# The last of twelve expert passes with the former pass' down products among its gate products, and the last layer's choices added ahead of the late products

## The chip, the cores and the metric

One Trainium2 chip, one NeuronCore. The core has TensorE (PE, matrix products and transposes into the PSUM banks), VectorE (DVE), ScalarE (ACT), GpSimd (POOL) and SyncE (SP), each with an instruction stream of its own, and DMA queues that the streams feed. The streams meet only at semaphores. The metric is the device time of one launch in microseconds (us), as the median of several runs.

## The reference

A two-layer encoder over 528 positions (16 meta tokens and 512 frames) of width 1024: a retention layer, then a sliding-window attention layer, each followed by a mixture of 16 experts, and a final norm.

```python
def hier_moe(h, w_group, w_router, w_gate, w_up, w_down):
    ...
    weights = g_w * top_p / jnp.sum(top_p, axis=-1, keepdims=True)
    expert_idx = g_sel[:, None] * EXPERTS_PER_GROUP + top_i
    gates = jnp.sum(jax.nn.one_hot(expert_idx, N_EXPERTS, dtype=jnp.float32) * weights[..., None], axis=1)
    a = jnp.einsum('td,edf->tef', t, w_gate)
    u = jnp.einsum('td,edf->tef', t, w_up)
    hid = jax.nn.silu(a) * u * gates[:, :, None].astype(t.dtype)
    y = jnp.einsum('tef,efd->td', hid, w_down)
    return y.reshape(b, l, d)

def reference(...):
    ...
    for i in range(DEPTH):
        ...
        h = h + hier_moe(rms_norm(h, moe_norm[i]), ...)
    return rms_norm(h, final_norm)[:, CHUNK:]
```

So each position goes through two experts of one group, and `h` receives both results, each times its weight.

## The kernel before

Each layer's expert stage sends every position's normed row to two slots of a table in DRAM (`slot_rows`), sorted by expert. The slots are worked off in twelve passes (`ROUNDS` = 12, `PASSES`), each of 128 slots in up to four tiles of 32. A slot group is a "pair" (64 slots of one expert) or a "single" (32 more). The last pass, k = 11, holds four singles, and pass 10 holds two pairs.

A pass k is four pieces of PE work: `rows_to_features(k)` (8 transposes of the slot rows), `gate_up(k)` (L1083: 8 blocks of 128 features, 4 products each, gate and up halves side by side in one bank, 2 or 3 by turns), `hidden_to_features(k)` (L1090: 2 transposes of the hidden values into bank 5) and `down_project(k)` (L1102: 16 products into banks 6 and 7). The trace has two records for each of these products. Between them, ACT makes the tanh of the gate half (`tanh_of`, L1423), DVE the hidden values (`hidden`, L1914 and L1915), ACT copies the transposed hidden values (`hidden_of`, L1436), and the results are copied to `yo` half by ACT (`results_of`, L1444, bank 6), half by DVE (L1923, bank 7). ACT then stores them to the DRAM table `slot_out` (L1450), except for the last pass. PE runs the passes one step apart: gate_up(k), hidden_to_features(k-1), rows_to_features(k+1), down_project(k-1).

The last pass' results are never stored. Instead `late_results` (L1135) multiplies them on PE by a one-hot matrix with the weights in it, one tile of positions after the other (meta tile first in the first layer, then 0 to 3), and DVE adds that to `h` (`add_late`, L1956). All other results are gathered back from `slot_out` by POOL (L2215, an indirect DMA for each of the two choices of each tile, into `gat`), once the stores of passes 9 and 10 have landed. DVE adds them with their weights (`first_choice` and `second_choice`, L1940 through `weighted`). The buffers of the gathered rows of tiles 2 and 3 lie over memory that expert weights used; before tile 3's gathers POOL waits for the last down products (bank 7).

POOL's stream is one queue: after the gathers of tile 2 it waits in the first layer for the square sum of the meta tile and makes its 1/rms (L2147, L2150, `deviations`), and only then gathers for tile 3. In the first layer DVE's order after the passes is: late add of the meta tile, its two choices, late adds of tiles 0 and 1, norm of the meta tile (L1556), first choice of tile 0, features of the meta tile for the keys and values (`kv_features`, L1562), second choice of tile 0, both choices of tile 1, norm of tile 0, and so on. PE goes on with the transposes of the normed tiles (L833) and the key and value products (`key_values`, L1149); tile 0's transposes stand halfway through the meta tile's products. In the last layer DVE adds the late product of tile t+1 behind the choices of tile t; ACT's square sum (L1287), POOL's 1/rms and DVE's final norm (L2121) follow for each tile, and SP stores the output.

SP loads, during the passes, the experts' next weights: the down weights of pass 10 (L684) go out when down_project(8) is done. In the first layer's last pass SP also issues the small tables of the attention stage (L799, `attention_loads`), once gate_up(11) and down_project(10) are both done. POOL has conditional weight loads of its own (L680, L684) that stand ahead of its gathers.

## Time and profile before

| | |
|---|---|
| median of 3 runs | 1138.62 us (1138.2 to 1141.27) |
| profiled execution | 1140.07 us, of which its span is 1138.4 us |
| mean granted TensorE clock | 0.972 |
| PE busy | 1050.2 us, 92% of the span |
| DVE / ACT / POOL busy | 446.1 / 263.5 / 240.5 us |
| chain that ended last | PE 79%, DVE 12%, issue 3%, DMA 2%, ACT 2%, POOL 1% |
| last pass and what follows, first layer | from 668.95 us to 757 us of the span |
| last pass and what follows, last layer | from 1091.92 us to the end |

The shares of the chain tell which engine's work the end waited for. PE holds most of it, but the two places that the change touches lie where the chain leaves PE: after the last pass of each layer it goes through a store, gathers, DVE and ACT. Those stretches are read there, row by row. A row of the timeline gives the start, the duration, the engine, the line and what ended the idle time ahead of it in brackets.

### The profile page before, as it was taken

What the parts mean: (1) busy time and instruction counts of PE and PEld (TensorE: products, weight loads), DVE (VectorE), ACT (ScalarE), POOL (GpSimd) and SP (SyncE); (2) the same over time, 40 slices, a digit from 0 to 9 for tenths busy, and PEclk for the clock granted to TensorE, in tenths of its full rate; (3) what the DMA queues carried; (4) which work ended last, traced back from release to release, by engine and by line L of the source; (5) the groups of instructions that cost most, each with busy time, mean ns of one, the idle gap of its engine ahead of it and who ended that gap; (6) DMA issues with size and microseconds to landing.
All of it is one profiled execution on the core that took longest, in us unless ns stands there. A gap on an engine that the chain in (4) does not pass through costs nothing.

```text
span 1138.4 us, 16440 instructions
## 1 busy us (share of the span) xinstructions
PE 1050.2 (92%) x6553; PEld 662.3 (58%) x6553; DVE 446.1 (39%) x806; ACT 263.5 (23%) x528; POOL 240.5 (21%) x232
## 2 busy tenths in 40 slices
PE   4999999999999999978999998989998978999982
PEld 4989979989988877753333332454444443333321
DVE  6400314224226540155132226557547745232216
ACT  5132143134224411020011111314214510111111
POOL 5333314205214533003000005510000002000004
PEclk9999999999999999988999998989999998999997
DMA  7232223114115121367899887030004058998945
GB/s 305 74 130 75 75 90 114 56 42 161 56 37 168 37 74 74 148 278 285 313 358 376 353 361 259 42 148 0 1 1 148 1 233 339 333 380 323 403 189 222
DMA packets 34838, 201.01 MB, mean 177 GB/s; under 512 B 4352, under 2 KB 4352, under 8 KB 25808
## 3 DMA queue, kind: packets, MB, share of 16 engines
q1 hardware_dynamic: 21168, 151.26, 34.7%
q10 hardware_dynamic: 8864, 31.74, 7.9%
q0 software_dynamic: 4736, 17.04, 4.1%
q8 instruction: 48, 0.79, 0.3%
q14 instruction: 22, 0.18, 0.0%
HBM read 303.70 MB, written 28.44 MB: 292 GB/s over the span
## 4 chain that ended last, share of the span: by engine, by line
PE 79%; DVE 12%; issue 3%; DMA 2%; ACT 2%; POOL 1%; SPq 0%; POOLq 0%; DVEq 0%; ACTq 0%
PE ps L844 30%; PE ps L1083 15%; PE ps L1102 7%; PE ps L969 4%; PE ps L1207 4%; PE ps L1149 3%; PE ps L850 3%; DVE arena L2079 2%; PE ps L1071 2%; DVE arena L2076 2%; PE ps L1060 1%; PE ps L912 1%; ACT arena L1522 1%; PE ps L1167 1%; DMA ring<-in_w_ret 1%
## 5 line engine op out<-in xcount | busy, mean ns | idle before, releaser
L844 PE MATMUL ps<-x_hi,ring_r 128*128 128x264 f32 x1024 | 190.9, 287 | 3.2 <-DVE xT L1562 3.1
L2159 POOL TENSOR_TENSOR ring_r<-ring,ring_r 128x1024 fp32r<-128x1024 f32 x56 | 136.9, 2459 | 260.5 <-ACT ring_r L1299 260.4
L844 PEld LDWEIGHTS ps<-x_hi,ring_r 128*128 128x128 f32 x1024 | 160.3, 190 | 3.6 <-issue 3.3
L1083 PE MATMUL ps<-arena,xT 128*32 128x512 f32 x864 | 158.0, 600 | 0.0
L1083 PE MATMUL ps<-ring,xT 128*32 128x512 f32 x672 | 143.9, 602 | 5.9 <-DVE xT L1562 5.9
L844 PE MATMUL ps<-xT_r,ring_r 128*128 128x264 f32 x512 | 146.2, 286 | 0.0
L1562 DVE TENSOR_TENSOR xT<-ps,gains 128x512 f32<-128x512 f32 (+1 forms) x76 | 46.9, 660 | 182.8 <-PE ps L1071 177.3
L844 PE MATMUL ps<-ring_r,x_hi 128*128 128x512 f32 x320 | 100.6, 395 | 0.0
L844 PEld LDWEIGHTS ps<-xT_r,ring_r 128*128 128x128 f32 x512 | 97.0, 189 | 0.1
L1102 PE MATMUL ps<-arena 128*32 128x512 f32 x624 | 87.3, 595 | 4.3 <-ACT arena L1436 4.3
L1299 ACT ACTIVATE ring_r<-ring 128x1024 fp32r<-128x1024 f32 x56 | 57.9, 1054 | 118.4 <-PE ps L844 70.8
L1083 PEld LDWEIGHTS ps<-arena,xT 128*32 128x32 f32 x864 | 41.6, 111 | 54.9 <-issue 54.4
L1083 PEld LDWEIGHTS ps<-ring,xT 128*32 128x32 f32 x672 | 38.1, 111 | 60.8 <-issue 60.3
L844 PEld LDWEIGHTS ps<-ring_r,x_hi 128*128 128x128 f32 x320 | 60.1, 188 | 13.9
L2147 POOL TENSOR_SCALAR var<-ss 128x1 f32<-128x1 f32 (+1 forms) x23 | 8.5, 371 | 239.7 <-ACT arena L1287 231.6
L1167 PE MATMUL ps<-ring,xT 128*128 128x512 f32 x128 | 56.1, 595 | 0.0
L1287 ACT ACTIVATE arena<-h 128x1024 f32<-128x1024 f32 (+1 forms) x23 | 24.3, 1057 | 102.7 <-DVE h L1940 48.0
L1436 ACT ACTIVATE arena<-ps 128x256 f32<-128x256 f32 x24 | 9.2, 385 | 167.5 <-PE ps L1090 162.9
L969 PE MATMUL ps<-arena 128*128 128x264 f32 (+4 forms) x256 | 47.8, 334 | 0.0
L1102 PEld LDWEIGHTS ps<-arena 128*32 128x32 f32 x624 | 22.8, 109 | 42.9 <-issue 41.3
L1522 ACT ACTIVATE arena<-arena 128x256 f32<-128x256 f32 x64 | 31.6, 494 | 62.6 <-DVE arena L2084 62.6
L969 PEld LDWEIGHTS ps<-arena 128*128 128x128 f32 (+1 forms) x256 | 41.1, 189 | 6.8
(265 smaller groups left out, 1554.7 us busy)
## 6 DMA issues: line engine op xcount, KB each, us to landing
arena<-in_w_gu SPq DMA_DIRECT2D x22, 2048.0 KB, 14.8
ring<-in_w_gu SPq DMA_DIRECT2D x20, 2048.0 KB
arena<-in_w_down SPq DMA_DIRECT2D x36, 1024.0 KB
arena<-in_w_gu POOLq DMA_DIRECT2D x18, 2048.0 KB
ring<-in_w_gu POOLq DMA_DIRECT2D x14, 2048.0 KB
arena<-in_w_down POOLq DMA_DIRECT2D x26, 1024.0 KB
ring<-in_w_ret SPq DMA_DIRECT2D x48, 512.0 KB, 3.7
ring<-in_w_ret_out SPq DMA_DIRECT2D x16, 512.0 KB, 4.9
```

Source lines behind the costliest of these rows:

```text
L844: last = mm(dst, a_parts[x], b_parts[y], start=(start and n == 0), stop=(stop and n == 2))
L850: last = mm(dst, both, part, start=(start and n == 0), stop=(stop and n == 1))
L969: last = mm(ps[:, b + g, c - lo:HALF], v_tm[0:r, t, 128 * m:128 * m + 128], scores_of(t)[0:r, c - 128 * t:hi - 128 * t], start=(t == 0), s ...
L1083: last = mm(ps[cols, b, :], xgT[:, k % 2, c, cols], by_row(gu(j))[:, c, :], start=(c == 0), stop=(c == KT - 1))
L1102: last = mm(ps[cols, b, :], hidT[:, c, cols], down(j)[:, c, 512 * n:512 * n + 512], start=(c == 0), stop=(c == 1))
L1149: last = mm(ps[0:rows(t), b, :], xTk[:, k, col0(t):col0(t) + rows(t)], w_kv[:, k, :], start=(k == 0), stop=(k == KT - 1))
L1167: last = mm(ps[:, b, :], xT[:, k, col0(t):col0(t) + 128], w_q[c][:, k, :], start=(k == 0), stop=(k == KT - 1))
L1207: last = mm(ps[:, b + c, :], oT1[:, k, :], w[:, k, :], start=(k == 0), stop=(k == KT - 1))
L1299: nc.scalar.activation(w_hi[to][:, m], w_raw[slot][:, m], ACT.Copy).then_inc(hi_made, 1)
L1522: nc.scalar.activation(P[:, hd, :], P[:, hd, :], ACT.Exp, bias=nmx[:, hd:hd + 1], accum_out=sm[:, hd:hd + 1]).then_inc(p_exp, 1)
L1562: return V_.tensor_tensor(dst[:, 4 * g:4 * g + 4, c0:c0 + r], src, gains[:, gain, 4 * g:4 * g + 4].unsqueeze(2).to_broadcast([128, 4, r]), ...
L2159: G.tensor_tensor(w_lo[slot][:, m], w_raw[slot][:, m], w_hi[to][:, m], ALU.subtract).then_inc(lo_made, 1)
```

## The change

Four edits, in both layers unless said otherwise.

1. PE's last pass is written in another order. Its gate products come in three pieces: blocks 0 to 2, then hidden_to_features(10), blocks 3 and 4, then down_project(10), then blocks 5 to 7. The pass' bank is told full after the last of them.
2. ACT and DVE follow: ACT makes the last tanh after it has stored pass 10's results, and DVE makes the last hidden values after it has copied pass 10's half.
3. In the last layer DVE adds both choices of a tile first and its late product behind them, so that the square sum of ACT waits for the late add. Before the late add DVE waits for its own second choice.
4. POOL waits for the last gate products (bank 3) before the gathers of tile 2.

```diff
@@ gate_up and the order of PE's passes
-                def gate_up(k):
+                def gate_up(k, blocks=range(KT)):
                     b = gu_bank(k)
-                    weights_arrived(pe, gu_in, gu_again, l, k)
-                    round_read(pe, l, B_ROWS, k)
-                    if k >= 2:
-                        round_read(pe, l, b, k - 2)
-                    for c in range(KT):
+                    if blocks[0] == 0:
+                        weights_arrived(pe, gu_in, gu_again, l, k)
+                        round_read(pe, l, B_ROWS, k)
+                        if k >= 2:
+                            round_read(pe, l, b, k - 2)
+                    for c in blocks:
...
-                    last.then_inc(full[b], 1)
+                    if blocks[-1] == KT - 1:
+                        last.then_inc(full[b], 1)
...
                 for k in range(1, ROUNDS):
+                    if k == ROUNDS - 1:
+                        gate_up(k, range(0, 3))
+                        hidden_to_features(k - 1)
+                        gate_up(k, range(3, 5))
+                        down_project(k - 1)
+                        gate_up(k, range(5, KT))
+                        break
                     gate_up(k)
                     hidden_to_features(k - 1)
@@ ACT
                     hidden_of(k - 1)
-                    tanh_of(k)
+                    if k < ROUNDS - 1:
+                        tanh_of(k)
                     results_of(k - 1)
+                    if k == ROUNDS - 1:
+                        tanh_of(k)
...
-            squares(MOE_TILES[1], nrm["_f"], next_junk, lambda t: act.wait_ge(mo[1]["gath_used"], t + 1))
+            squares(MOE_TILES[1], nrm["_f"], next_junk, lambda t: fl.wait_read(act, f"LC1_{t}"))
@@ DVE
+                    if k == ROUNDS - 1:
+                        results_of(k - 1)
                     hidden(k)
-                    results_of(k - 1)
+                    if k < ROUNDS - 1:
+                        results_of(k - 1)
...
                     dve.wait_ge(m[f"gathered{t}"], 32)
-                    fl.wait_read(dve, f"LC{l}_{t}")
+                    if l == 0:
+                        fl.wait_read(dve, f"LC{l}_{t}")
...
-            add_late(0)
             for t in range(NT):
                 first_choice(t)
                 second_choice(t)
-                if t + 1 < NT:
-                    add_late(t + 1)
+                dve.wait_ge(mo[1]["gath_used"], t + 1)
+                add_late(t)
                 if t == 1:
                     final_norm(0)
@@ POOL
                     r = rows(t)
+                    if t == 2:
+                        round_full(pool, l, gu_bank(ROUNDS - 1), ROUNDS - 1)
                     if t == NT - 1:
                         round_full(pool, l, B_YB, ROUNDS - 1)
```

How PE's order moves, in the last layer's last pass (the first layer's is the same). Lines 1083, 1090 and 1102 of before are 1084, 1092 and 1104 of after; `ring` and `arena` hold the weights. Before, from the last of the eight gate blocks on:

```order
L1083 MATMUL ps<-ring,xT 32x512
L1083 MATMUL ps<-arena,xT 32x512 x3
L1090 MATMUL ps<-con,arena 128x128 [waits bank_free2]
L1090 MATMUL ps<-con,arena 128x128
L1102 MATMUL ps<-arena 32x512 [waits bank_free5,bank_free6,down_in3,down_in2]
L1102 MATMUL ps<-arena 32x512
L1102 MATMUL ps<-down_rows,arena 32x512 x2
```

After, from the third of the eight gate blocks on:

```order
L1084 MATMUL ps<-ring,xT 32x512
L1084 MATMUL ps<-arena,xT 32x512 x3
L1092 MATMUL ps<-con,arena 128x128 [waits bank_free2]
L1092 MATMUL ps<-con,arena 128x128
L1084 MATMUL ps<-ring,xT 32x512
L1084 MATMUL ps<-arena,xT 32x512 x3
L1084 MATMUL ps<-ring,xT 32x512
L1084 MATMUL ps<-arena,xT 32x512 x3
L1104 MATMUL ps<-arena 32x512 [waits bank_free5,bank_free6,down_in3,down_in2]
```

The transposes of pass 10's hidden values and its down products have moved ahead of the last three gate blocks, and two gate blocks stand between them.

DVE's order in the last layer, from its last pass to the second tile. Before:

```order
L1914 SCALAR_TENSOR_TENSOR arena<-arena,ps 128x256 [waits tanh_done_1]
L1915 SCALAR_TENSOR_TENSOR arena<-arena,ps 128x256 [waits dve_steps_moe1]
L1923 COPY arena<-ps 128x512 [waits y_out0_1,bank_full7]
L1923 COPY arena<-ps 128x512 [waits y_out1_1,bank_full7]
L1956 TENSOR_TENSOR h<-ps,h 128x1024 [waits bank_full0,final_gain_in]
L1940 SCALAR_TENSOR_TENSOR h<-arena,h 128x1024 [waits bank_free0,gathered0_1]
L1940 SCALAR_TENSOR_TENSOR h<-arena,h 128x1024 [waits dve_steps_moe1]
L1956 TENSOR_TENSOR h<-ps,h 128x1024 [waits bank_full2]
```

After:

```order
L1935 COPY arena<-ps 128x512 [waits y_out0_1,bank_full7]
L1926 SCALAR_TENSOR_TENSOR arena<-arena,ps 128x256 [waits tanh_done_1]
L1927 SCALAR_TENSOR_TENSOR arena<-arena,ps 128x256 [waits dve_steps_moe1]
L1935 COPY arena<-ps 128x512 [waits y_out1_1,bank_full7]
L1955 SCALAR_TENSOR_TENSOR h<-arena,h 128x1024 [waits gathered0_1,final_gain_in]
L1955 SCALAR_TENSOR_TENSOR h<-arena,h 128x1024 [waits dve_steps_moe1]
L1972 TENSOR_TENSOR h<-ps,h 128x1024 [waits bank_full0,gath_used_1]
```

Pass 10's copy now stands ahead of the last hidden values, and the first late add behind the first tile's choices.

## Rows read from the trace of the kernel before

**Rows 1.** Chain that ended last, first layer: start us, us, what

```profile
668.95 6.87 PE ps L1083 x64
...
681.34 5.75 DMA slot_out<-arena
```

**Rows 2.** Timeline of SP, first layer's last pass: start, duration, engine, line, operation

```profile
680.62 0.33 SPq L799 DMA_DIRECT2D arena<-in_t_swa  x1
```

**Rows 3.** Timeline of POOL behind the first layer's store

```profile
687.89 0.87 POOL L2215 DMA_INDIRECT xT<-slot_out,slot_g  x1 [6.56 <-DMA slot_out<-arena]
...
697.87 0.18 POOL L2147 TENSOR_SCALAR var<-ss 16x1 f32<-16x1 f32 x1
...
698.88 2.67 POOL L2215 DMA_INDIRECT arena<-slot_out,slot_g  x1 [0.19 <-issue]
```

**Rows 4.** Timeline of DVE behind the first layer's passes

```profile
688.90 1.21 DVE L1956 TENSOR_TENSOR h<-ps,h 16x1024 f32<-16x1024 f32 x1 [2.17 <-PE ps L1135]
691.92 2.58 DVE L1940 SCALAR_TENSOR_TENSOR h<-xT,arena,h 16x1024 f32<-16x1024 f32 x2 [1.80 <-DMA xT<-slot_out,slot_g]
694.43 2.34 DVE L1956 TENSOR_TENSOR h<-ps,h 128x1024 f32<-128x1024 f32 x2
698.73 0.74 DVE L1556 TENSOR_SCALAR arena<-h,rstd 16x1024 f32<-16x1024 f32 x1 [1.97 <-POOL rstd L2150]
...
705.19 0.75 DVE L1556 TENSOR_SCALAR arena<-h,rstd 128x1024 f32<-128x1024 f32 x1 [0.46 <-POOL rstd L2150]
```

**Rows 5.** Timeline of ACT there: the meta tile's square sum

```profile
694.53 1.06 ACT L1287 ACTIVATE arena<-h 16x1024 f32<-16x1024 f32 x1 [9.60 <-DVE h L1940]
```

**Rows 6.** Timeline of PE there: late products, transposes, key and value products

```profile
686.99 8.94 PE L1135 MATMUL ps<-arena,short 128*16 128x512 f32 x20 [1.00 <-DVE arena L1923]
699.62 1.00 PE L833 MATMUL ps<-con,arena 16*128 16x16 f32 x8 [3.69 <-DVE arena L1556]
701.16 5.91 PE L1149 MATMUL ps<-ring,arena 128*16 128x512 f32 x8 [0.54 <-DVE arena L1562]
707.00 1.09 PE L833 MATMUL ps<-con,arena 128*128 128x128 f32 x8
```

**Rows 7.** Stretches there: us, busy by engine, PE clock, DMA share, GB/s

```profile
699.00:700.00 1.00, 0.38 (x4) 0.41 (x5) 1.00 (x2) 0.00 (x0) 1.00 (x1) 0.51 0.86 348
```

**Rows 8.** Line 684, 640 to 712 us: the load of pass 10's down weights and its landing

```profile
L684 SPq DMA_DIRECT2D down_rows<-in_w_down x1: 747/747/747, 658.2 to 658.2; - x1
...
DMA to landing us min/median/max: 11.1/11.1/11.1
```

**Rows 9.** Chain that ended last, last layer

```profile
1091.92 6.87 PE ps L1083 x64
1098.79 0.38 PE ps L1090 x2
...
1099.84 3.67 PE ps L1102 x32
...
1104.31 2.61 DMA slot_out<-arena
...
1108.98 6.77 DMA arena<-slot_out,slot_g
```

**Rows 10.** Timeline of the last layer's last pass, PE, ACT and DVE

```profile
1099.48 0.38 ACT L1423 ACTIVATE arena<-ps 128x256 f32<-128x256 f32 x1
...
1100.34 0.42 DVE L1915 SCALAR_TENSOR_TENSOR arena<-arena,ps 128x256 f32<-128x256 f32 x1
...
1105.32 0.63 PE L1102 MATMUL ps<-arena 128*32 128x512 f32 x3 [1.48 <-ACT arena L1436]
```

**Rows 11.** Timeline of DVE, last layer: choices, late add, final norm of the first tile

```profile
1115.78 2.60 DVE L1940 SCALAR_TENSOR_TENSOR h<-arena,h 128x1024 f32<-128x1024 f32 x2 [2.54 <-DMA arena<-slot_out,slot_g]
...
1118.30 1.22 DVE L1956 TENSOR_TENSOR h<-ps,h 128x1024 f32<-128x1024 f32 x1
...
1123.29 1.28 DVE L2121 SCALAR_TENSOR_TENSOR arena<-h,rstd,arena 128x1024 f32<-128x1024 f32 x1
```

## The prediction

> **What bounds the kernel now.** I read the page first: PE is busy for 92% of the span and holds most of the chain that ended last, so what moves other engines matters only where that chain leaves PE. The chain, followed in order of time, leaves it at two places that the change touches: behind pass 10's down products in the first layer [rows 1] and in the last [rows 9]. In both it goes DVE copy, store of pass 10, POOL's gathers, DVE. From there I read the timelines of each engine [rows 2 to 6, 10, 11]. The reader should see three things. In the first layer PE stands idle for 3.69 us between the late products and the transposes of the meta tile, and the products behind that run slowly, 5.91 us for 8 records [rows 6], at a granted clock of 0.51, the lower of the two levels (1.2 GHz), reached in that idle time [rows 7]. What ended the idle time is the meta tile's norm on DVE, which waited for POOL's 1/rms [rows 4], and POOL came to that only when eight gathers were out: 687.89 to 697.87, 9.98 us [rows 3]. In the last layer DVE waits for the first gather until 1115.78 and is then busy nearly without a gap to the end [rows 11].
>
> **The last pass on PE.** I take the last layer's times; the first layer's pass is the same, 422.97 earlier (668.95 against 1091.92) [rows 1, 9]. The eight gate blocks take 6.87, so 0.86 each. Before: gate 1091.92 to 1098.79, transposes 0.38, down products of pass 10 from 1099.84, 3.67 long, to 1103.51 [rows 9]. So 0.67 of stall stood ahead of them, for ACT's copy of the hidden values. After: three blocks 2.58, transposes 0.38, two blocks 1.72 (which hide ACT's copy, 0.67), so the down products start at 1096.6 and end at 1100.2 to 1100.3: **3.3 us earlier**. No row shows a bank left with an open sum while others are written, except the meta tile's key and value products, with another tile's transposes in their middle [rows 6]; nothing stands idle there, so I take nothing for it (0 to 0.3).
>
> The last three blocks end at 1102.8. Now the hidden values of pass 11 have no cover. From the tanh's start to their end is 1.28 (1099.48 to 1100.34 + 0.42) [rows 10], some 0.2 passes until PE starts, and transposes, copy and wait take 1.05 as before (1098.79 to 1099.84) [rows 9]: the last down products start at 1105.4, against 1105.32 [rows 10]. Two stalls of PE, 0.67 and 1.48 [rows 10], have been exchanged for one of 1.5 and one of 0.67. **PE: +0.1 us.** ACT now has the store ahead of the tanh; the store is issued at 1101.0, 1.8 before the tanh can run, so that costs nothing, unless the copies of banks 6 and 7 come 1.5 later.
>
> **The store and the gathers.** The store followed the down products' end by 0.80 (1103.51 to 1104.31) [rows 9], so it goes out at 1101.0 in the last layer and at 678.0 in the first. In the last layer it took 2.61 [rows 9]; in the first 5.75 [rows 1], after SP had issued the attention tables at 680.62 [rows 2], ahead of the store at 681.34. SP waits for the last gate products too, which now end at 679.9, so the tables go out 1.9 after the store instead of 0.7 before it. Its length is between 2.61 and 5.75; I take 2.61, since the tables come last now. First gather 0.80 after landing (681.34 + 5.75 = 687.09 to 687.89) [rows 1, 3]: at 681.4, or 684.6 at the other end, against 687.89.
>
> POOL's new wait for the last gate products (679.9) is over before the first gather; the wait for the last down products (682.4 + 3.7 = 686.1) before it gets to tile 3. Both are free.
>
> **First layer, on DVE.** The late add of the meta tile moves by PE's +0.1 to 689.0 and ends at 690.2. The two choices began at 691.92 after 1.80 of idle, waiting for the gather [rows 4], 4.03 after the first gather's start. With the new start that landing is 685.4 to 688.6, in either case before DVE is free, so they run from 690.2 to 692.7 and DVE does the two late adds until 695.05. Beside it ACT makes the square sum, 1.06 and some 0.2 around it [rows 5], till 693.95; POOL is through its eight gathers at 691.4 (or 694.6) and takes 0.86 (697.87 to 698.73) [rows 3, 4]: 694.8 (or 695.5). So the meta tile's norm runs at 695.1 instead of 698.73, now bound by DVE's own queue. PE started 0.89 after that norm (699.62) [rows 4, 6]: 696.0. The late products end at 686.99 + 8.94 + 0.1 = 696.0 [rows 6]: PE's idle time is gone, and that is also the limit of what can be got there.
>
> Next is tile 0. DVE needs 6.46 from the meta norm to tile 0's norm (698.73 to 705.19) [rows 4], which comes at 701.55, and PE can start tile 0's transposes 0.89 later, at 702.45. PE itself would be there earlier: without the idle time the clock should stay at the upper level, and 8 records then take 8 x 0.447 = 3.6 (8.94 over 20 records) [rows 6] instead of 5.91, so from 697.55 to 701.1. Against 707.00 [rows 6] the gain is **4.5 us**. If the clock falls all the same, PE is there at 703.5: 3.5. If DVE is quicker than before, 701.1 is the floor: 5.9. From here on to 757 us PE works without a gap in the chain, so what is gained is kept.
>
> **Last layer, on DVE.** The first gather landed at 1108.98 + 6.77 = 1115.75 [rows 9]. Everything ahead of it moves by 3.3, the load of the final gains too, so 1112.45. Then DVE has, tile by tile, two choices 2.60 and a late add 1.22 [rows 11], and one final norm in between. Before, three late adds lay behind the first landing, since the first one was done while DVE waited; now four do: +1.22. The new waits for DVE's own second choice cost what the wait between two choices costs, which is next to nothing (2.60 for two) [rows 11]: 0.1 to 0.4 for four. The first late product was added before DVE's idle time began, at 1115.78 - 2.54 - 1.22 = 1112.0 [rows 11], and the others follow 1.8 apart (8.94 for five) [rows 6]; now the first add comes at 1115.1 and they 3.8 apart, so none is late. Together +1.4, net **1.9 us** gained. What follows the last tile (square sum, 1/rms, final norm, store) is as before.
>
> **The sum** is 4.5 + 1.9 = 6.4 us. The profiled execution took 1140.07, so it would be 1133.7; that execution lay 1.45 above the median of 1138.62, and against the median the forecast is **1132.2**. The ends of the terms: first layer 3.2 to 5.9, last layer 1.3 to 2.3.
>
> **A rule weighed against a row.** In the first layer tile 3's gather took 2.67, with DVE's norm of the meta tile beginning 0.15 earlier [rows 3, 4]. The Trainium skill, "SBUF — State Buffer", section "Who interferes with whom", says that a DVE tensor_scalar in its two-port mode and GpSimd lock each other out, and that "Issue order, not op shape, decides who blocks". The long gather agrees with that. Now POOL is done with the 1/rms at 694.8 and issues tile 3's gather at once, ahead of the norm, which waits for DVE until 695.1. By that rule the norm would have to wait for the gather.
>
> **The rivals.** (B) That turn of order costs the meta norm what it cost the gather: 2.67 against the 0.87 of a quick one [rows 3], up to 1.8, once. The sum is 4.6: 1134.0. (C) In the first layer gathers and tables crowd each other, and the meta tile's gathers land no earlier than 691.9: only the clock and part of POOL's queue are gained, 2: 1134.7. For it speaks that the store was slow in such company [rows 1, 2], against it that the meta tile's gathers are small (16 rows) and have until 690.2, 8.8 us from their start. (D) In the last layer the landings of the gathers are set by other traffic, so DVE gains nothing there and pays the 1.4: 4.5 - 1.4 = 3.1: 1135.5. Against it: the traffic before the gathers is that of before, 3.3 earlier. (E) Slower: pass 10's down products stand 3.2 us earlier, and their weights are not there. They landed at 658.2 + 11.1 = 669.3 [rows 8] and are wanted at 673.6, so there are 4.3 us to spare. Beyond that each us s stalls PE, in both layers, since gate blocks and the last down products queue behind: 6.4 - 2s. No gain is left at s = 3.2, and the kernel is slower by more than 0.3% from s = 4.9, say 1142.2 at s = 5. Nothing new is loaded, so this would need a much later landing than this trace has. (F) The change doesn't do what it says, since another wait than PE's order holds pass 10's results (the store of pass 8, bank 7): all went by without idle time in the passes before; 1138 to 1140.
>
> **How the numbers follow.** Forecast 0.68, B 0.10, C 0.10, D 0.07, E 0.03, F 0.02. The range goes from the upper ends of the terms (1138.62 - 8.2 = 1130.4) to a little over D: 1130.3 to 1136.0. With 0.3% (3.4 us, about what a measurement of this kernel can tell from no change) the line lies at 1135.2. Nearly all of the forecast and B, half of C and D are below it: faster 0.85, same 0.12, slower 0.03.
>
> **What the profile of the changed kernel would show.** Pass 10's down products start 4.7 after the last gate products' start, and the last pass as a whole ends within 0.2 of before. Both stores are issued 3.3 earlier and both take about 2.6. In the first layer PE's idle time between late products and meta transposes is under 0.5, the clock stays at 1.00 in that stretch, and 8 records of the key and value products take 3.6. In the last layer the first choice starts 20.5 us after the last pass' gate products, and the last late add ends 16.7 us later, with no idle time of DVE over 0.1 in between. I would be wrong if the store took 5 us in the last layer, if the meta norm still waited for POOL, or if DVE in the last layer waited for gathers of tiles 1 to 3.

## The result, and the profile after

| | before | after |
|---|---|---|
| median of 5 runs each | 1138.2 us (1137.3 to 1141.27) | 1133.22 us (1131.95 to 1133.78) |
| profiled execution | 1140.07 us, span 1138.4 | 1133.78 us, span 1132.1 |
| mean granted TensorE clock | 0.972 | 0.973 |
| PE / DVE busy | 1050.2 / 446.1 us | 1051.0 / 446.2 us |

The ratio is 0.9946, with a 95% interval of 0.9932 to 0.9959: 5 us or 0.5% faster. Between the two profiled executions the span fell by 6.3 us, against 6.4 in the forecast. The medians fell by 5.0. The total is close, but the first layer gave about a microsecond less and the last layer about a microsecond more than forecast, and these cancel. To see it, each stretch is timed from the start of the last pass' gate products of its layer (S0 in the first, S1 in the last), since S0 itself varies by up to 3.3 us between profiles of kernels that are alike up to there. S0 and S1 are the starts of the first gate record in PE's timeline (668.77 and 1091.74 before, 668.87 and 1088.47 after); the chain puts that start 0.2 later, and the forecast's 4.7 counts from there.

| us from S0, first layer | before | forecast | after |
|---|---|---|---|
| pass 10's down products start | 8.1 | 4.7 | 4.8 |
| late products start | 18.2 | 18.3 | 19.7 |
| store of pass 10 is issued | 12.6 | 9.2 | 9.3 |
| first gather | 19.1 | 12.6 to 15.8 | 13.2 |
| meta tile's choices | 23.2 | 21.4 | 23.4 |
| meta tile's norm | 30.0 | 26.3 | 28.2 |
| tile 0's transposes | 38.2 | 33.7 | 35.8 |
| S1 - S0 | 423.0 | 418.5 | 419.6 |

| us from S1, last layer | before | forecast | after |
|---|---|---|---|
| first gather | 16.0 | 12.7 | 12.7 |
| first choice | 24.0 | 20.7 | 19.8 |
| last square sum starts | 39.2 | 37.3 | 36.2 |
| end of the span | 46.7 | 44.8 | 43.6 |

So the first layer gave 3.4 instead of 4.5, and the last 3.0 instead of 1.9. Of the 3.4, only 2.5 was there at tile 0's transposes, where the forecast had its 4.5. The chain that ended last of the kernel after, first layer, in order of time (start, us, engine or DMA, tile and line); lines 1104, 1955, 1972 and 2232 of after are 1102, 1940, 1956 and 2215 of before:

```profile
669.05 2.58 PE ps L1084 x24
...
673.85 3.48 PE ps L1104 x32
...
678.13 3.13 DMA slot_out<-arena
...
683.24 9.05 DMA xT<-slot_out,slot_g
692.31 1.28 DVE h L1955
...
697.27 2.67 POOL arena L2232
...
703.75 0.76 DVE arena L1568
```

The store now takes 3.13 instead of 5.75 [rows 1], but behind it the chain holds a 9.05 us transfer that it did not hold before: the meta tile's second gather, 64 KB. DVE's timeline there:

```profile
690.48 1.21 DVE L1972 TENSOR_TENSOR h<-ps,h 16x1024 f32<-16x1024 f32 x1 [2.17 <-PE ps L1144]
692.31 2.58 DVE L1955 SCALAR_TENSOR_TENSOR h<-xT,arena,h 16x1024 f32<-16x1024 f32 x2 [0.62 <-DMA xT<-slot_out,slot_g]
...
697.11 0.74 DVE L1568 TENSOR_SCALAR arena<-h,rstd 16x1024 f32<-16x1024 f32 x1
```

The choices begin at 692.31, later than the 691.92 of [rows 4], although the gather was issued 5.8 earlier. DVE still waits for the gather there. Only the wait for POOL's 1/rms (1.97 in [rows 4]) is gone: the norm of the meta tile has no idle time ahead of it. What was in the gather's way shows in the DMA issues of 676 to 706 us (KB each, median us from issue to landing). Before:

```profile
arena<-in_swa_b_o SPq DMA_DIRECT2D x1, 512.0 KB, 8.7
...
xT<-slot_out,slot_g POOLq DMA_INDIRECT x2, 3.1
```

After:

```profile
arena<-in_swa_b_o SPq DMA_DIRECT2D x1, 512.0 KB, 10.1
...
xT<-slot_out,slot_g POOLq DMA_INDIRECT x2, 8.3
```

The attention tables, 1.8 MB issued by SP at 680.0 to 682.0, now fall on the gathers instead of on the store. The last table was issued at 682.00, landed 10.1 later at 692.1. Of the meta tile's two gathers the first, issued at 682.06, landed at 689.6, and the second, for which the choices wait, at 692.3.

The other error is on PE. Its timeline in the first layer's last pass and behind it:

```profile
681.27 0.44 PE L1092 MATMUL ps<-con,arena 128*128 128x128 f32 x2 [1.41 <-DVE arena L1927]
682.37 1.08 PE L1104 MATMUL ps<-arena 128*32 128x512 f32 x3 [0.67 <-ACT arena L1445]
...
684.05 1.10 PE L1104 MATMUL ps<-arena 128*32 128x512 f32 x3
...
685.65 0.62 PE L1104 MATMUL ps<-arena 128*32 128x512 f32 x3
...
688.56 8.94 PE L1144 MATMUL ps<-arena,short 128*16 128x512 f32 x20 [1.01 <-DVE arena L1935]
698.00 0.64 PE L833 MATMUL ps<-con,arena 16*128 16x16 f32 x8 [0.50 <-DVE arena L1568]
699.46 3.59 PE L1158 MATMUL ps<-ring,arena 128*16 128x512 f32 x8 [0.82 <-DVE arena L1574]
704.65 1.07 PE L833 MATMUL ps<-con,arena 128*128 128x128 f32 x8 [1.59 <-DVE arena L1568]
```

The two stalls, 1.41 and 0.67, are those of the forecast. What came on top is that the first four of the eight groups of last down products take 0.93 to 1.10 for three records instead of 0.63 [rows 10], because the clock fell. Stretches of the kernel after (us, busy by engine in the order PE, PEld, DVE, ACT, POOL with how many instructions, PE clock, DMA share, GB/s):

```profile
682.00:683.00 1.00, 0.63 (x4) 0.23 (x8) 0.00 (x0) 0.12 (x1) 0.87 (x1) 0.56 0.77 299
683.00:684.00 1.00, 1.00 (x8) 0.23 (x4) 0.00 (x0) 0.00 (x0) 0.77 (x1) 0.50 0.36 124
...
686.00:687.00 1.00, 1.00 (x16) 0.27 (x8) 0.00 (x0) 0.50 (x1) 0.69 (x2) 1.00 0.84 234
...
699.00:700.00 1.00, 0.54 (x2) 0.22 (x3) 1.00 (x4) 0.00 (x0) 0.94 (x1) 1.00 0.00 0
```

From 0.56 at 682 to 0.50 and back to 1.00 at 686: the lower level, 1.2 GHz, for some 3.5 us. The last row answers to [rows 7]: there, where before the clock was at 0.51, it is now up, and the meta tile's 8 records take 3.59 instead of 5.91 [rows 6].

In the last layer the chain reads:

```profile
1097.73 2.61 DMA slot_out<-arena
...
1101.13 0.97 POOL arena L2232
1102.40 5.71 DMA arena<-slot_out,slot_g
1108.22 1.29 DVE h L1955
...
1123.40 1.23 DVE h L1972
1124.66 1.06 ACT arena L1296
```

and DVE's timeline:

```profile
1107.34 0.69 DVE L1935 COPY arena<-ps 128x512 f32<-128x512 f32 x1 [6.52 <-PE ps L1104]
1108.22 2.60 DVE L1955 SCALAR_TENSOR_TENSOR h<-arena,h 128x1024 f32<-128x1024 f32 x2 [0.18 <-DMA arena<-slot_out,slot_g]
1110.86 1.22 DVE L1972 TENSOR_TENSOR h<-ps,h 128x1024 f32<-128x1024 f32 x1
```

The first choice starts right behind the copy of pass 11's results, which itself is late because of the slow clock. Only 0.18 us is left of the 2.54 us wait of [rows 11].

### The profile page after: what moved, and what is told of

The parts are those of the page before. It is cut to its first block, busy times and chain, and to the rows that moved or that the text cites. A ratio compares the mean times of both kernels' runs of the same rounds, so it can differ in the third digit from the quotient of the medians.

```text
span 1132.1 us, 16440 instructions
## 1 busy us (share of the span) xinstructions
PE 1051.0 (93%) x6553; PEld 662.8 (59%) x6553; DVE 446.2 (39%) x806; ACT 263.5 (23%) x528; POOL 241.0 (21%) x232
## 4 chain that ended last, share of the span: by engine, by line
PE 78%; DVE 12%; DMA 3%; issue 3%; ACT 2%; POOL 1%; SPq 0%; POOLq 0%; DVEq 0%; ACTq 0%
PE ps L844 31%; PE ps L1084 15%; PE ps L1104 7%; PE ps L969 4%; PE ps L1216 4%; PE ps L1158 3%; PE ps L850 3%; DVE arena L2095 2%; PE ps L1071 2%; DVE arena L2092 2%; PE ps L1060 1%; PE ps L912 1%; ACT arena L1534 1%; PE ps L1176 1%; DVE h L1955 1%
## 5 line engine op out<-in xcount | busy, mean ns | idle before, releaser
L1104 PE MATMUL ps<-arena 128*32 128x512 f32 x624 | 90.4, 612 | 1.3 <-ACT arena L1445 1.3
L1104 PE MATMUL ps<-down_rows,arena 128*32 128x512 f32 x144 | 46.6, 619 | 0.0
```

The costliest lines, as they stand in the source:

```text
L1104: last = mm(ps[cols, b, :], hidT[:, c, cols], down(j)[:, c, 512 * n:512 * n + 512], start=(c == 0), stop=(c == 1))
```

## The experiments

Each kernel was timed against the kernel before on the same chip; ratios come with their 95% interval. Times from S0 and S1 are from one profile of each.

### One layer at a time

```diff
-                    if k == ROUNDS - 1:
+                    if l == 0 and k == ROUNDS - 1:     # first_layer_only; l == 1 in last_layer_only
```

The same condition guards the orders of ACT and DVE. In `first_layer_only` edit 3 is left out too. Edit 4 stays in both layers.

> The new order of the last pass (PE, ACT, DVE) in the first layer alone; the last layer's pass and its adds are as before. Theory: the two layers' gains are separate and add up. In the changed kernel's profile the last layer's last pass starts 3.3 us earlier than before's (1088.65 against 1091.92), so this kernel should be 3.3 us below before, some 1135, and its last layer should take from the last pass' gate products to the end what before's takes, 46.5 us. Rival: the gain seen between the layers (2.4 us up to tile 0's transposes, 0.9 more around 761 us of the span, where PE's products ran faster) is half chance of the clock: then 2.4 us.

> The new order of the last pass in the last layer alone, with the adds in the new order; the first layer's pass is as before. Theory: 3.0 us below before (the stretch from the last pass' gate products to the end took 46.48 us in before and 43.45 in the changed kernel), some 1135.3. Rival: the gather's shorter landing (6.98 us from its issue in place of 8.05) was chance, then 1.9 us.

Measured: `first_layer_only` 1136.45 against 1138.74, ratio 0.9974 (0.9965 to 0.9983), S1 - S0 419.2, the last layer as before (47.0). `last_layer_only` 1136.75, ratio 0.9982 (0.9971 to 0.9993), S1 - S0 423.3, and 43.5 from S1 to the end. Each layer keeps its gain alone, and in the profiles they are 3.8 to 4.1 and 3.2, near equal, where I had forecast more than twice as much for the first. The medians give less, 2.3 and 2.0. They are the figures of the two rivals (2.4 and 1.9), but the intervals, 1.9 to 4.0 and 0.8 to 3.3, hold the gains of the profiles too, so the medians don't decide between theory and rival. Together they make 4.3, against 5.0 of the whole change in its own comparison.

### The order of the adds

`adds_alone` is the kernel before with edit 3 alone, `adds_as_before` the kernel after without it:

```diff
+            add_late(0)
             for t in range(NT):
                 first_choice(t)
                 second_choice(t)
-                dve.wait_ge(mo[1]["gath_used"], t + 1)
-                add_late(t)
+                if t + 1 < NT:
+                    add_late(t + 1)
```

> The changed kernel with the last layer's adds in the old order (late product of tile 0 first, then choices). Theory: the first gather lands at 19.5 us after the last pass' gate products, but the first late product is only ready at 21.4 and its add ends at 22.7, so DVE starts the choices 3.1 later than in the changed kernel and has one add less behind them (1.2): 1.9 us above the changed kernel. Rival, if the order of adds only moves work around: 1.2 us below it.

> Before with the adds of the last layer in the new order and nothing else. Theory: DVE waits for the first gather anyway, and the first late add, which was hidden in that wait, now stands behind it: 1.2 to 1.4 us above before, 1139.5. Rival: no difference, if another engine (ACT's square sum and POOL's 1/rms, or the output stores) hides it.

Measured: `adds_alone` 1140.14, ratio 1.0014 (1.0005 to 1.0023), slower than before by 1.6 us (0.6 to 2.6). Its DVE timeline shows why:

```profile
1116.21 2.60 DVE L1940 SCALAR_TENSOR_TENSOR h<-arena,h 128x1024 f32<-128x1024 f32 x2 [5.35 <-DMA arena<-slot_out,slot_g]
1118.85 1.22 DVE L1957 TENSOR_TENSOR h<-ps,h 128x1024 f32<-128x1024 f32 x1
```

The wait has grown from 2.54 to 5.35, and the late add that used to fill it stands behind the landing. From first choice to last square sum it took 16.45 instead of 15.19: +1.26, of which 1.22 is that add, so the added waits cost next to nothing.

`adds_as_before` has pass 10 early and the old order of adds: 1135.55, ratio 0.9966 (0.9952 to 0.998).

```profile
1108.04 0.69 DVE L1935 COPY arena<-ps 128x512 f32<-128x512 f32 x1 [6.56 <-PE ps L1104]
1111.05 1.23 DVE L1971 TENSOR_TENSOR h<-ps,h 128x1024 f32<-128x1024 f32 x1 [2.31 <-PE ps L1144]
1112.38 2.61 DVE L1955 SCALAR_TENSOR_TENSOR h<-arena,h 128x1024 f32<-128x1024 f32 x2
```

Here DVE waits 2.31 for PE's late product, and only then comes the first choice, at S1 + 23.25 against 19.75 after. The end comes 45.9 after S1 instead of 43.6: 2.2 us. So edit 3 costs 1.3 by itself and gains 2.2 once the gather lands before the first late product. It is worth having only together with the early store.

The 2.2 holds a part of the slow clock's price: the clock fell in this profile too (late products at S1 + 19.85), and the old order waits for those products. With the clock up they start 1.7 earlier (18.16 in `fill`, below). The old order could then start its choices at about 21.6, the new one at 19.94, and with the add of 1.25 behind it, edit 3 would gain some 0.4 us. That is an estimate from these profiles; no run tested it.

### Fill, and the tables out of the way

`fill` gives PE two products into a free bank behind the last gate products, their results unused; they hold PE for some 1.5 us, until the last hidden values are there. `tables` issues the five attention tables behind the first layer's last gather. `fill_tables` has both.

```diff
                         gate_up(k, range(5, KT))
+                        fl.wait_read(pe, f"OT{l}_{tiles[-1]}")
+                        mm(ps[:, 4, :], ident, con[:, 0:512], start=True, stop=True)
+                        mm(ps[:, 4, 0:256], ident, con[:, 0:256], start=True, stop=True)
@@ tables
             sp.wait_ge(mo[0]["gathered3"], 32)
+            for dst, src in (...):                     # the loop of attention_loads, moved
+                sp.dma_start(dst, src).then_inc(s_swat, 16)
```

> The changed kernel with two products of no use (512 and 256 columns, into a free bank, about 1.3 us) on PE behind the last gate blocks, where PE stood idle for 1.41 us. Theory: the granted clock fell to 0.50 in the last down products because the idle time ahead of them grew; with it filled the clock stays at 1.00, the last down products take 3.6 us in place of 5.1 in both layers, and the late products start 1.5 earlier. The time hardly changes (0 to 0.6 us less), since in the first layer the meta tile's gather lands 0.6 after DVE is free and in the last one the first gather lands after the copy of the last results. Rival: the clock falls for another reason (what PE did before, not its idle time), and the last down products stay at 5.1.

> The changed kernel with SP's five attention tables (1.8 MB) issued only when all gathers of the first layer have landed, instead of in the last pass. Theory: the meta tile's gather took 9.05 us to land because the tables' transfers ran beside it; without them it lands in about 4 us, DVE starts the meta tile's choices right behind its late add (691.7 in place of 692.3), and the gain is 0.6 us, bound then by PE's slow last down products. Rival: POOL's own other gathers delay it, and the landing stays at 8 to 9 us.

> Both: PE's idle time filled and the tables late. Theory: the two bounds of the meta tile (its late add after PE's last down products, its gather's landing) lie 0.6 us apart, so only both together give more: the late add starts at 689.0 and the choices at 690.2, which is 2.1 us less than in the changed kernel; 1131. Rival: DVE's or POOL's queue in the first layer takes it back, 0.5 us or less.

Measured: `fill` 1133.35 against 1138.49, ratio 0.996 (0.9947 to 0.9973), the same as after. PE did what I wanted of it:

```profile
680.43 0.63 PE L1104 MATMUL ps<-arena 128*32 128x512 f32 x3 [0.67 <-ACT arena L1448]
...
685.08 8.94 PE L1147 MATMUL ps<-arena,short 128*16 128x512 f32 x20 [1.00 <-DVE arena L1938]
```

All last down products run at 0.63, and the late products start 18.2 after S0 and S1. But DVE waits the longer for the gather:

```profile
686.99 1.21 DVE L1975 TENSOR_TENSOR h<-ps,h 16x1024 f32<-16x1024 f32 x1 [2.17 <-PE ps L1147]
690.13 2.58 DVE L1958 SCALAR_TENSOR_TENSOR h<-xT,arena,h 16x1024 f32<-16x1024 f32 x2 [1.93 <-DMA xT<-slot_out,slot_g]
```

The meta tile's choices come at S0 + 23.21, where after has 23.44. In the last layer the first choice comes at S1 + 19.94 with a wait of 2.03 for the gather, where after has 19.75. The 1.5 us of PE was real, and taking it away gained next to nothing, because the gathers now held DVE until about the same time.

`tables` 1133.82, ratio 0.9955 (0.9942 to 0.9968). Its DVE timeline:

```profile
688.70 1.21 DVE L1971 TENSOR_TENSOR h<-ps,h 16x1024 f32<-16x1024 f32 x1 [2.17 <-PE ps L1143]
690.02 2.58 DVE L1954 SCALAR_TENSOR_TENSOR h<-xT,arena,h 16x1024 f32<-16x1024 f32 x2
...
694.83 0.74 DVE L1567 TENSOR_SCALAR arena<-h,rstd 16x1024 f32<-16x1024 f32 x1
```

No wait for the gather is left. The choices come at S0 + 21.40 and tile 0's norm at 32.84, where the forecast had 21.4 and 32.8. The gain is more than the 0.6 us that I expected, for a reason that isn't the tables: in this profile the clock stayed up in the first layer (late products at S0 + 18.16). It has to be compared not with after but with the profiles with the clock up, `fill` and `after_again` (below), with choices at 23.21 and 23.19: 1.8 us. With the clock down the late add ends at S0 + 22.8, as in after (690.48 + 1.21), and only 0.6 would be gained. That the gathers themselves got quicker shows in the DMA issues of `fill_tables`, which has the filler too:

```profile
xT<-slot_out,slot_g POOLq DMA_INDIRECT x2, 2.6
```

That is 2.6 us from issue to landing, against a median of 7.6 in `fill`, which differs in the place of the tables alone. So the tables' traffic is what the gathers had waited for. Of the 2 us won there 0.8 to 1.0 is left in S1 - S0 (418.6 against 419.3 in `after_again` and 419.6 in after), and the median shows none of it: the attention's first tile takes longer again. `fill_tables`, 1131.9, ratio 0.9933 (0.9919 to 0.9946), has the same marks and the best median of the three, but the intervals overlap.

### How the store's time passes through

`early_fill_tables` is `fill_tables` with pass 10's pieces as early as they go, `later_split` is the kernel after with them later:

```diff
-                        gate_up(k, range(0, 3))
+                        gate_up(k, range(0, 1))        # later_split: range(0, 5)
                         hidden_to_features(k - 1)
-                        gate_up(k, range(3, 5))
+                        gate_up(k, range(1, 2))        # later_split: range(5, 7)
                         down_project(k - 1)
-                        gate_up(k, range(5, KT))
+                        gate_up(k, range(2, KT))       # later_split: range(7, KT)
```

> As fill_tables, with pass 10's down products moved still further ahead: behind one gate block, its transposes and one more block, 2.57 us earlier. Theory: in the last layer the first gather lands 2.6 us earlier, but DVE first has to copy the last pass' results, which with the clock kept up ends 1.6 us earlier than in the changed kernel; the first choice can start 1.6 to 2 us earlier, so 1.6 to 2 us below fill_tables; the first layer gains nothing more, since the late product of the meta tile binds it. Rival: pass 10's down weights, which land some 1.7 us before the products that need them, come too late, and PE stalls: no gain or a loss.

> The changed kernel with pass 10's down products two gate blocks later (blocks 0 to 4, transposes, 5 and 6, down products, 7), which is 1.72 us. Theory: the end follows the store one for one in the last layer (DVE's chain hangs on the first gather): the stretch from the last gate products to the end grows by 1.7 to some 45.3 us; in the first layer the meta tile's choices hang on the tables' and gathers' traffic and move by 0 to 0.6. In all 1.7 to 2.3 us above the changed kernel, and still 4 below before. Rival, by my forecast's account of the first layer (late add of the meta tile is the bound): only the last layer moves. PE's idle time ahead of the last hidden values stays 1.4, so the clock falls as in the changed kernel.

Measured: `later_split` 1135.49 against 1139.26, ratio 0.9964 (0.9951 to 0.9976). Its down products start 1.7 later. The first layer does not feel it: choices at S0 + 23.31, S1 - S0 419.5. In the last layer all of it arrives, and more: the end comes 45.8 after S1 instead of 43.6. There DVE waits again:

```profile
1107.53 0.69 DVE L1935 COPY arena<-ps 128x512 f32<-128x512 f32 x1 [6.38 <-PE ps L1104]
1110.26 2.64 DVE L1955 SCALAR_TENSOR_TENSOR h<-arena,h 128x1024 f32<-128x1024 f32 x2 [2.05 <-DMA arena<-slot_out,slot_g]
```

`early_fill_tables` 1131.06, ratio 0.9936 (0.9923 to 0.9949): down products at S0 + 2.2, first choice at S1 + 18.1 instead of 20.1 in `fill_tables`, end at 41.9 instead of 44.0; S1 - S0 unchanged at 418.6. So the last layer follows the store, though not one for one: 1.7 us later cost 2.1 to 2.3, 2.6 us earlier gave 2.0. The medians of `fill_tables` and `early_fill_tables` differ by 0.8 and their ratios not at all, so this last gain is seen in the profiles alone. The first layer gains nothing, and not only because the late add binds it. The store is issued at S0 + 6.7 instead of 9.3, but takes 5.9 us instead of 3.5, and the first gather comes at S0 + 13.4 instead of 13.5. The tables are out of the way in both kernels, but the store now starts among the loads ahead of it: the DMA engines move 360 to 475 GB/s from 675 to 679 us. That fits its length; no run tests it apart. The rival, down weights that come too late, did not show: PE has no idle time ahead of pass 10's down products. In `later_split` PE's idle time ahead of the last hidden values' transposes was 1.76, not the 1.4 expected, and the clock fell in the last layer only.

### The kernel after again, the final gains late, and all together

`after_again` is the kernel after, unchanged. `gains_late` starts the load of the final gains after tile 1's gathers, and DVE waits for it only ahead of the first final norm:

```diff
+            sp.wait_ge(mo[1]["gathered1"], 32)
             sp.dma_start(fin_g, a["final_norm"].partition_broadcast(128)).then_inc(fin_in, 16)
...
-            dve.wait_ge(fin_in, 16)
             def final_norm(t):
+                if t == 0:
+                    dve.wait_ge(fin_in, 16)
...
-                if t == 1:
+                if t == 2:
                     final_norm(0)
```

`best` has the early pieces, `fill`, `tables` and `gains_late`.

> The changed kernel once more, unaltered, for a second profile of it on the chip of the next three. Theory of the stretches: from the first layer's last gate products to the last layer's 419.2 to 419.6 us, from there to the end 43.4 to 43.7 us, the granted clock at 0.50 in the last down products of at least one layer. Rival: the gather's shorter landing was chance, and this profile's last stretch is 44.5 us or more.

> The changed kernel with SP's load of the final gains (512 KB) held back until the gathers of tile 1 have landed, and the first final norm put behind tile 2's adds. Theory: that load runs beside the first gather, so without it the gather lands about 1.2 us earlier (512 KB at some 400 GB/s), but DVE has the copy of the last results until 19.2 us after the gate products, so it can start at most 0.5 earlier: 0.5 us less. Rival: POOL's other gathers fill the DMA engines anyway, and the landing stays between 5.6 and 6.1 us from the second issue.

> Everything that helped: pass 10's down products behind two gate blocks, PE's idle time filled, the attention tables behind the first layer's gathers, the final gains behind tile 1's gathers. Theory: first layer to last layer 418.6 us, then 41.4 to 41.9: 3 us below the changed kernel, 9 below before, some 1129.5. Rival: only what either alone gave, 1131.

Measured: `after_again` 1133.41 against 1139.26, ratio 0.995 (0.9937 to 0.9962), the same as after. In its profile the clock did not fall in the first layer, and the late products started at S0 + 18.2 instead of 19.7. Still the meta tile's choices came at 23.19:

```profile
688.09 1.21 DVE L1972 TENSOR_TENSOR h<-ps,h 16x1024 f32<-16x1024 f32 x1 [2.17 <-PE ps L1144]
691.21 2.58 DVE L1955 SCALAR_TENSOR_TENSOR h<-xT,arena,h 16x1024 f32<-16x1024 f32 x2 [1.91 <-DMA xT<-slot_out,slot_g]
```

So without the clock's fall the gather alone holds the choices. In `first_layer_only` it is the other way round: the clock fell, the second gather landed at 689.3 (7.7 after its issue at 681.60), and DVE goes from the late add to the choices without a wait for it:

```profile
688.58 1.21 DVE L1973 TENSOR_TENSOR h<-ps,h 16x1024 f32<-16x1024 f32 x1 [2.17 <-PE ps L1144]
689.90 2.58 DVE L1957 SCALAR_TENSOR_TENSOR h<-xT,arena,h 16x1024 f32<-16x1024 f32 x2
```

That is S0 + 22.98; `adds_as_before` has 23.18 in the same way. With the clock's fall the late add ends at S0 + 22.8 to 23.1 in the three profiles that have it; the second gather lands at S0 + 22.4 to 23.5 in all seven that have the tables ahead of it; the forecast had 21.4. Each hides the other's price: the clock's fall costs the first layer 0.25 at most as long as the gathers are late, and by these ends it would cost about 1.4 (22.8 against 21.4) once they are not.

`gains_late` 1133.6, ratio 0.9949 (0.9936 to 0.9962): the same as `after_again`. The first choice starts directly behind the copy, at S1 + 19.40 instead of 19.63. With DVE's queue as the bound, this run can't tell how much earlier the gathers land without the load beside them.

`best` 1129.93 (1126.45 to 1131.38), ratio 0.9916 (0.9903 to 0.993): 9.3 us below the kernel before and 3.5 below `after_again` on the same chip, with intervals of the ratios that don't overlap. Its last layer ends 41.7 after S1. Its span of 1124.8 is partly luck: S1 - S0 is 416.4, where three kernels with the same marks up to the attention's first tile (89.15 to 89.19 after S0) have 418.6, and nothing was changed in between.

## Why the prediction was right, and where it was wrong

**Total and sign: right, and in the closeness of the total lucky.** 1132.2 forecast, 1133.22 measured, the span 6.3 shorter for 6.4. Of the 4.5 us forecast up to tile 0's transposes, 2.0 were missing; 0.9 came back in the attention and 1.1 in the last layer, and the forecast had a reason for neither. The reasoning that PE's order matters through the store held: the last layer moves with it in `later_split` and `early_fill_tables`.

**Pass 10's down products 3.3 earlier, and no cost of the open sum: right.** 8.09 to 4.79 after S0, 8.1 to 4.8 in the last layer; three blocks 2.58 and the down products 3.48 in the chain. POOL's new wait was free, as said: the gathers of tile 2 follow the others after 0.30 us. The store took the forecast's 2.61 in the last layer, but 3.1 to 3.7 in the first in every profile with the pieces where the change has them, also where the tables were moved away (3.7 in `tables`). So not the tables cost it that half microsecond and more; what did is open.

**PE +0.1: wrong, +1.5.** The step that failed is "Two stalls of PE, 0.67 and 1.48, have been exchanged for one of 1.5 and one of 0.67". The stalls came out as said, but I gave them no effect on the clock. Turned round, with only two transposes between them, they were followed by a fall of the granted clock to 0.50. This was so in the last layer of all seven profiles of the new order without filler, and in three of seven in the first layer. It was so in none of six layers in the old order, and in none of eight with filler. The same stalls were followed by a fall in one profile and not in another of the same kernel (after and `after_again`, first layer), so what decides it is open. In after the price was nearly hidden in both layers, because the gathers landed late enough: `fill` takes it away and gains nothing that is clear of noise. In `first_layer_only` it is what held the meta tile's choices.

**First layer 4.5: wrong, 2.5 at tile 0's transposes, 3.4 in S1 - S0.** The failed step is the landing of the meta tile's gathers, "at 685.4 to 688.6, in either case before DVE is free". It was 692.3. I had taken the distance from the first gather to the landing, 4.03, from [rows 3, 4], where the last table had been issued 5.5 us ahead of the gather. I had written myself that the tables now go out behind the store, and drew from it only that the store gets quicker. I did not go on to ask what they meet next. That is rival C. It had 0.10, because small gathers with 8.8 us of time seemed safe; its "no earlier than 691.9" was right, its 2 us of gain too low. `tables` and `fill_tables`, both with the clock up in the first layer, give the forecast's marks from the choices to tile 0's transposes to within 0.15.

**The clock stays up in the meta tile's products: right** (1.00; 3.59 instead of 5.91). PE's idle time before the meta transposes was 0.50, about as said, but by luck: the late products ended 1.5 late themselves, and where they did not, it was 1.78 (`after_again`). Before tile 0's transposes stood 1.59, where the forecast had 1.35 (701.1 to 702.45); `tables` has 1.60. A part of the gain appears only later: in the kernels with the old order in the first layer the attention's first tile takes 43.9 in each of three profiles, in those with the new one 42.9 to 43.5 (44.1 where the tables are moved as well, 43.7 in `best`). In the chains that ended last a row of PE there is, before:

```profile
762.85 2.06 PE ps L1224 x7
```

and after:

```profile
760.06 1.52 PE ps L1233 x7
```

The clock is at 0.50 from about 761 us in both, and in after a part of these seven products runs ahead of that. Why the clock stays up that far there was not tested.

**Rival B, the norm behind the gather: didn't happen, not excluded.** The norm of the meta tile began at 697.11, tile 3's gather at 697.27, again 2.67 long. The order of [rows 3, 4] was not turned, and being later than forecast is not the reason: in `tables`, where both come when the forecast had them, the norm begins at 694.83 and the gather at 694.98. In all fourteen profiles the norm is first by 0.15 or 0.16, so the forecast's 0.3 the other way was wrong, and the case in which the gather goes first wasn't met. The long gather is weaker support for the rule than the forecast took it for: in after the next gather took 2.30 as well (1.18 before), with DVE in the choices and no norm beside it.

**Last layer 1.9: too low, 3.0.** The late add behind the landing cost 1.25 (16.44 from first choice to last square sum, 15.19 before), of the 1.4 forecast. The gathers were issued 3.31 earlier, as forecast. But the first choice came another 1.0 earlier, 7.1 after the first issue (1101.13 to 1108.22) instead of 8.1 (1107.71 to 1115.78). The term of the sum that was mis-sized is "everything ahead of it moves by 3.3": the first choice moved by 4.3. For that distance, profiles of the old order in the last layer have 7.3 to 8.5. Those of the new one have at most 6.7 to 7.4, but 8.0 in `early_fill_tables` and up to 7.7 in `best`. The two ranges overlap, and no run settles the cause; a part of it may be chance.

## What to carry to other kernels

When a transfer is moved away from a burst of loads, follow the burst: write down what is issued in the 10 us behind it and who waits for that. Look ahead of it as well: moved 2.6 us further forward, the first layer's store ran into the loads before it and landed no earlier. Where two late operands meet at one instruction, removing one of them shows nothing; take both away before calling either free. An order of adds should be chosen by which operand lands first, and chosen again when a change moves the landings: the same edit cost 1.3 us alone and gained 2.2 beside the early store with the slow clock.

## What the runs showed of the hardware

**Small gathers beside large loads.** Two indirect gathers of 64 KB took a median of 3.1 us from issue to landing when the last of the tables' loads (1.8 MB) was issued 5.5 us ahead of them, and 8.3 when it was issued just before. Without the tables beside them it was 2.6 (`fill_tables`). In between lies `later_split`, 6.8 with the last table 2.0 us ahead. In after the first gather landed at 689.6 and the second at 692.3, with the last table at 692.1. The Trainium skill, "DMA: Bandwidth & Descriptors", section "Queues, rings and completion order", says that a semaphore increment lands only after every earlier write of the same DMA engine, across its queues. The second gather lands 0.2 us behind the last table, which would fit, but the first lands 2.5 ahead of it, though issued 0.06 behind it. The traces don't show in what order a DMA engine took up the writes, so no run here shows whether their order or the shared bandwidth makes the gathers late.

**The clock can fall on two short stalls.** Idle times of 1.42 and 0.67 us, with two transposes of 0.44 between, were followed by down products at the lower level in the last layer of all seven profiles with the new order there and no filler (in `later_split` the first idle time was 1.76). In the first layer the same stalls had that effect in three profiles of seven. After:

```profile
1100.87 0.44 PE L1092 MATMUL ps<-con,arena 128*128 128x128 f32 x2 [1.42 <-DVE arena L1927]
1101.98 1.07 PE L1104 MATMUL ps<-arena 128*32 128x512 f32 x3 [0.67 <-ACT arena L1445]
```

In the old order the stalls of 0.67 and 1.48 us [rows 9, 10] had 3.67 us of down products between them, and no fall followed. With 1.5 us of products in the first of the two gaps the clock stayed up in all eight cases. What tells the cases with a fall from those without is not known.
